# Group loads of the expert-value stage in four pieces, one behind each weight load

## The reference, cut to what matters

```python
act = jax.nn.gelu(jnp.einsum('cd,ced->ce', xc, expert_u[ic]), approximate=False)
return jnp.einsum('ce,ced->cd', (gc * act).astype(xc.dtype), expert_v[ic])
```

## Time and profile before

| | |
|---|---|
| time, median of 3 runs | 4268.71 us (4264.19 to 4283.66) |
| the profiled execution, span | 4269.1 us |
| TensorE matmul busy | 4033.2 us (94%) |
| VectorE busy | 2519.8 us (59%) |
| GpSimd busy | 2309.5 us (54%) |
| ScalarE busy | 1502.1 us (35%) |
| value stage, from its first matmul to its last | 3127 to 4244 us |
| DMAs from the stream, 1024 KB each | 396 |
| DMAs of gates, 704 KB each | 32 |
| DMAs of activations, 704 KB each | 32 |

### The profile page before, as it was taken

The page is one execution under the profiler, slowest core; times in us unless marked ns, Lnnn a source line. Parts: engine busy times, 40 slices in busy tenths (PEclk is TensorE's granted clock), DMA queues, the critical chain, the costliest instruction groups (busy, mean ns, idle before and its releaser), DMA issues.

```text
span 4269.1 us, 70172 instructions
## 1 busy us (share of the span) xinstructions
PE 4033.2 (94%) x27233; PEld 3579.2 (84%) x27233; DVE 2519.8 (59%) x3407; ACT 1502.1 (35%) x2053; POOL 2309.5 (54%) x930
## 2 busy tenths in 40 slices
PE   7999999999999999899998799999998999999997
PEld 5777777777788778699998799999988999999997
DVE  4344334444454552367773666667467788778775
ACT  4332323333322221233335766666322222222223
POOL 4332233333233443354555467667667888888774
PEclk9999999999999999999999999999999999999998
DMA  3222222222223343233334699999898999999893
GB/s 122 89 83 85 82 91 79 92 85 90 88 89 108 136 143 130 109 133 131 131 123 174 253 358 373 372 371 364 332 357 328 356 360 372 353 359 361 301 349 117
DMA packets 258397, 899.44 MB, mean 211 GB/s; under 512 B 107672, under 2 KB 140696, under 8 KB 162736
## 3 DMA queue, kind: packets, MB, share of 16 engines
q1 hardware_dynamic: 175984, 482.50, 32.0%
q0 software_dynamic: 46080, 335.56, 19.2%
q10 hardware_dynamic: 36160, 78.85, 4.8%
HBM read 828.10 MB, written 68.71 MB: 210 GB/s over the span
## 4 chain that ended last, share of the span: by engine, by line
PE 56%; issue 14%; POOL 9%; DMA 6%; ACT 5%; SPq 5%; DVE 3%; ACTq 1%; POOLq 0%; DVEq 0%
PE ps L389 14%; PE ps L391 13%; PE ps L390 13%; POOL wl L384 7%; DMA raw<-stream 5%; SPq L555 5%; PE ps L1985 2%; PE ps L1987 2%; PE ps L1986 2%; PE ps L1675 2%; ACT wh L380 2%; ACT stage L1038 1%; ACT oh L1033 1%; DVE stage L1470 1%; PE ps L1934 1%
## 5 line engine op out<-in xcount | busy, mean ns | idle before, releaser
L384 POOL TENSOR_TENSOR wl<-raw,wh 128x2048 fp32r<-128x2048 f32 x396 | 1834.6, 4633 | 1836.1 <-ACT wh L380 1835.7
L389 PE MATMUL ps<-xh,wh 128*128 128x352 f32 (+1 forms) x3904 | 1434.0, 367 | 37.6 <-DVE xl L1162 18.9
L391 PE MATMUL ps<-xh,wl 128*128 128x352 f32 (+1 forms) x3904 | 1400.8, 359 | 0.0
L390 PE MATMUL ps<-xl,wh 128*128 128x352 f32 (+1 forms) x3904 | 1399.3, 358 | 0.0
L380 ACT ACTIVATE wh<-raw 128x2048 fp32r<-128x2048 f32 x396 | 758.2, 1915 | 1595.1 <-PE ps L391 775.7
L389 PEld LDWEIGHTS ps<-xh,wh 128*128 128x128 f32 x3904 | 740.3, 190 | 133.6 <-issue 44.3
L391 PEld LDWEIGHTS ps<-xh,wl 128*128 128x128 f32 x3904 | 738.9, 189 | 83.4
L390 PEld LDWEIGHTS ps<-xl,wh 128*128 128x128 f32 x3904 | 740.4, 190 | 81.5 <-issue 7.7
L1985 PE MATMUL ps<-gah,wh 128*128 128x352 f32 x2048 | 682.7, 333 | 81.6 <-POOL wl L384 67.8
L1987 PE MATMUL ps<-gah,wl 128*128 128x352 f32 x2048 | 675.7, 330 | 0.0
L1986 PE MATMUL ps<-gal,wh 128*128 128x352 f32 x2048 | 674.0, 329 | 0.0
(11 more groups left out here) (333 smaller groups left out, 4020.1 us busy)
## 6 DMA issues: line engine op xcount, KB each, us to landing
raw<-stream SPq DMA_DIRECT2D x396, 1024.0 KB
gelu_scratch<-preb ACTq DMA_DIRECT2D x128, 176.0 KB
gates_scratch<-stage ACTq DMA_DIRECT2D x22, 1024.0 KB
gt<-gates_scratch SPq DMA_DIRECT2D x32, 704.0 KB
act<-gelu_scratch SPq DMA_DIRECT2D x32, 704.0 KB
mergegate_scratch<-sgb ACTq DMA_DIRECT2D x32, 256.0 KB, 2.1
sgm<-mergegate_scratch SPq DMA_DIRECT2D x32, 256.0 KB, 2.7
h_in<-x_t SPq DMA_DIRECT2D x4, 1024.0 KB, 9.0
```

Of the source, the lines that this page charges most:

```text
L384: pool.tensor_tensor(wl[s][:, :], raw[s][:, :], wh[s][:, :].bitcast(F32), ALU.subtract).then_inc(w_lo, 1)
L389: pe.matmul(dst, w_h, h[:, kx, lo:], start=start, stop=False)
L390: pe.matmul(dst, w_h, l[:, kx, lo:], start=False, stop=False)
L391: return pe.matmul(dst, w_l, h[:, kx, lo:], start=False, stop=stop)
```

## The change

`load_group` gets a part number. The gates are loaded in three pieces along their first axis (blocks 0 to 6, 7 to 13 and 14 to 21 of 22), the activations are the fourth piece. For a group g other than 0, the pieces of group g+2 are issued one behind each unit load of group g: gates behind c = 0, 1 and 2, activations behind c = 3. The waits that stood before the load (`gal_ready` of group g among them) now stand behind the unit load c = 0. For group 0 all four pieces stay together where the loads were, behind c = 2 (group 1) and c = 3 (group 2), and the load of group 0 itself is four pieces together. A group now raises `group_in` by 64, not 32. SP's loop over pairs of groups is written out (32 groups). The two raw buffers, and all that ACT, DVE, POOL and PE do, stay, but for the value that POOL waits for.

```diff
-            def load_group(g, s):
-
-                sp.dma_start(gt[s][:, :, :], gate_d[:, :, bass.ds(GE * g, GE), :].rearrange("b p e t -> p b (e t)")).then_inc(group_in[s], 16)
-                sp.dma_start(act_[s][:, :, :], act_d[bass.ds(GE * g, GE)].rearrange("e p t -> p e t")).then_inc(group_in[s], 16)
+            def load_group(g, s, part):
+                if part < 3:
+                    b = slice(GB * part // 3, GB * (part + 1) // 3)
+                    sp.dma_start(gt[s][:, b, :], gate_d[b, :, GE * g:GE * g + GE, :].rearrange("b p e t -> p b (e t)")).then_inc(group_in[s], 16)
+                else:
+                    sp.dma_start(act_[s][:, :, :], act_d[GE * g:GE * g + GE].rearrange("e p t -> p e t")).then_inc(group_in[s], 16)
...
-            load_group(0, 0)
+            for part in range(4):
+                load_group(0, 0, part)
...
                 for c in range(NC4):
                     load_unit(sp, U_PEER + NC4 * g + c, c % 2)
-                    if c == 3 and ahead:
+                    if c == 2 and first:
+                        sp.wait_ge(w_used, U_PEER)
+                        for part in range(4):
+                            load_group(1, 1, part)
+                    if c == (3 if first else 0) and ahead:
                         for r in range(2):
                             sp.wait_ge(pre_stored[r], 16 + 8 * NKEYS)
                         sp.wait_ge(gal_ready, GE * g + GE)
-                        load_group(g + 2, s)
-                    if c == 2 and first:
-                        sp.wait_ge(w_used, U_PEER)
-                        load_group(1, 1)
-
-            for s in range(2):
-                load_values(s, s, first=s == 0)
-            with sp.Fori(1, GROUPS // 2 - 1) as i:
-                for s in range(2):
-                    load_values(2 * i + s, s)
-            for s in range(2):
-                load_values(GROUPS - 2 + s, s, ahead=False)
+                    if ahead and (c == 3 or not first):
+                        for part in range(4) if first else (c,):
+                            load_group(g + 2, s, part)
+
+            for g in range(GROUPS):
+                load_values(g, g % 2, ahead=g < GROUPS - 2, first=g == 0)
...
             def gated(g, s, e):
-                pool.wait_ge(group_in[s], 16 * (g - s) + 32)
+                pool.wait_ge(group_in[s], 32 * (g - s) + 64)
```

## The result

The changed kernel takes 4256.2 us (median of 17), the kernel before, in the same rounds, 4274.0. The ratio is 0.9949, with a 95% interval of 0.9937 to 0.9961: 0.5% faster, where 1.1% was forecast. The time lies in the stated range; the gain is 18 us where 47 was forecast. Two of the 17 executions ran at a much lower granted clock (4932 and 5752 us at 0.75 and 0.63), and all ratios go by the others.

The account below looks back on a forecast made before the run. Late unit loads, queued behind the group load in one piece, were taken to bound the stage, not PE. 4269.1 - 50 (engines' share) + 3 (load of c = 1) = 4222 us; range for 8 in 10: 4190 to 4265.

Parts of the forecast that it names:

- What bounds the kernel: Value stage, groups 1 to 28: late unit loads set the pace, not PE; loss 115 us, DMA engines' work 897 us.
- The engines' term: Groups 1 to 28: smoothing raises the DMA share from 0.92 to 0.97, a gain of 50 us, bounds 21 to 78.
- (b): Load of c = 1, now behind the wait and first piece: 3 us added in all, bounds 0 to 53.
- (c): Groups before and after: group 0 keeps its loads and hold, groups 29 to 31 load nothing; cost 0.
- crowded case: Load of c = 1 beside gathers: packets take up to 7 us, landing at 11.0, PE loses 1.9 us a group.
- rival 3: At c = 0 the first piece holds SP as long as the whole did: 112 us slower, 4381; chance 0.07.
- (a): SP's queue: two more DMA issues a group, at most 1.3 us of SP's 34.8; cost nothing.
- (d): SP's loop written out: fewer register instructions, more instruction fetch; cost 0, bounds -1 to +2.
- (e): POOL's multiplications wait for four DMAs, not two; first use is some 20 us later, so no new wait.
- Rival 2: Engines already full: lateness spreads to all four units and the gathers, share stays 0.94; gain 19, 4250; chance 0.20.
- Rivals 1 and 4: First: engines can do more, only PE's pace is left, 4169, chance 0.08. Second: pieces bunch up as before, 4269, 0.03.
- The signs: Expected in the profile: L555 off the chain, ACT's 245 us of waits halved, clock 0.98, DMA share 0.96 to 0.98.

Follow-up runs that it names:

- one_later: Changed kernel with the wait and all pieces one unit load later (wait and first gates' piece behind c = 1); 4203.6 us, ratio to before 0.9824, repeat 0.9829.
- wait_alone: one_later with the wait behind c = 0 and the activations' piece issued before that wait; ratio to before 0.9874, repeat 0.9850.
- one_later_wait0: one_later with the wait behind c = 0 and the activations' piece after it, ahead of load c = 1; ratio to before 0.9976.
- two_at_0: Changed kernel with two gates' pieces behind c = 0, the third behind c = 1, activations behind c = 2; ratio to before 1.0032.
- group1_later: Changed kernel, but in group 1 alone the wait and first two gates' pieces stand behind c = 1; 4244.3 us, ratio to before 0.9928.
- split_only: Kernel before with the load cut in four pieces, all behind c = 3, and SP's loop written out; ratio to before 0.9980.
- act_first: Changed kernel with the activations' piece behind c = 0 and the gates' pieces behind c = 1, 2 and 3; ratio to before 0.9978.

## Why the prediction was wrong in size, point by point

**What bounds the kernel: right.** The stage was held by late units, not by PE, and the engines' work, 897 us, stayed (893). The chain and the DMA share gave it.

**The engines' term (-50): right in itself, but it is not this kernel's.** It says what well placed pieces bring. one_later has a share of 0.98 and gains 61.8 us in groups 1 to 28 (975.0 to 913.2), where I had put 50 and bounds of 21 to 78. The changed kernel reached 0.94 and 24.9 us; the 36.9 us between the two are the next terms, (b) and (c).

**The step that failed is (b), the load of c = 1, put at 3 us in all with bounds of 0 and 53. It measured 26.5 us over groups 2 to 28 (908.9 us against one_later's 882.4), and 36.9 us with group 1 (950.1 against 913.2).** What I wrote of its mechanism was there: the wait ends 0.4 us after the low half, the piece goes first. SP is not held for the 2.2 us that I had (a piece's issue takes 0.43 us in the median, as the row below shows), so the load is issued 0.9 us after its low half and not 3.2. But the piece's data goes ahead of the unit's, and the unit then takes 9.7 us to ACT, where I had 4.3 free and 7.8 crowded. Together that is 10.6 us in the median, near the 11.0 of my crowded case, not the 7.5 of the free one. The crowded case was the normal one, as the share of 0.92 said. I then took 3 us with the reason that the engines' shortage already counted it. That was upside down: the share comes out of the lateness. The 10.4 us of group 1 belong to (c) below. By the medians one_later is some 53 us faster; the profiled executions are 37 us apart, 4246.3 and 4209.4, since that of the changed kernel is the fastest of its 17 and that of one_later the slowest of its 5. That it was the piece behind the wait, and not the moving of all four, is shown by wait_alone against one_later_wait0 and by two_at_0. Two slips in the sum of (b) change nothing: 11.0 less 7.8 is 3.2, not 3.1, and the 2.5 us of slow clock in rival 3 stand in no row (rows 4 give 3.0).

The gates' pieces on SP's queue, all 96 (ns min/median/max; compare):

```profile
L555 SPq DMA_DIRECT2D gt<-gates_scratch x96: 367/434/14960, 3033.2 to 4116.3; - x96
```

**(c), no cost in the groups before and after: wrong in group 1.** I looked at where the pieces of group 0 stand and not at the wait of group 1, the first that stands at c = 0. There the last `gal` of group 1 comes late: POOL makes its last two products only at 3157.37 to 3159.23, and DVE takes a gathered row before the `gal` (SP's queue, DVE and PE, changed kernel):

```profile
3166.35 0.37 SPq L555 DMA_DIRECT2D gt<-gates_scratch  x1
3166.76 0.57 SPq L374 DMA_DIRECT2D raw<-stream  x1
...
3164.19 2.06 DVE L1487 TENSOR_TENSOR gal<-act,gah 128x352 fp32r<-128x352 f32 x2
...
3181.52 0.66 PE L1986 MATMUL ps<-gah,wh 128*128 128x352 f32 x1 [7.27 <-POOL wl L384]
```

The low half that releases the load of c = 1 ends at 3154.88, 11.9 us before the issue at 3166.76; PE stands 7.27 us and starts again at the lower clock (0.66 us a matmul). group1_later and the pairs of wait_alone and one_later put it at 8 to 9 us.

**(a), (d), (e) at nothing: right**, by split_only.

**The rivals.** Rival 2 (engines full, gain 19, 4250) is what the number looks like, but its reason falls: the engines were not full at 0.94, and PE's gaps stand mostly at c = 1, not at all four units. That it came within 6 us of the result is luck. The 358 GB/s of the Trainium skill's "DMA: Bandwidth & Descriptors" (section "Bandwidth"), which would have given 22 us of gain, is a like case: near the result by luck, and against the 379 GB/s that one_later moves over 710 us. I had left out that the same section gives this figure for two cores that stream from one memory; here one core runs. Rival 3 had the right place, the load c = 1, with the wrong mechanism, a hold of SP; two_at_0 shows that the same place can make the change slower than before. Rivals 1 and 4 did not come.

**The signs.** The hold at the activations' DMA left the chain, no piece in groups 2 to 23 held SP for more than 2.6 us, and the clock rose to 0.98, as written. The share stayed at 0.94, where 0.96 to 0.98 was written, and DVE's wait for gathers at 13.5 us (13.1 before). ACT's waits for units did not halve, they grew, and they are a poor sign: in one_later they are 282 us, at a gain three times as large.

**Open.** Group 29 takes 38.2 us in the profiled execution of the changed kernel and 37.2 in group1_later, which has the same order there; in before it takes 30.9, in one_later 33.8 and in act_first 32.4. In the changed kernel the loss is again at c = 1: the load is issued at 4109.40, 0.9 us after its low half, ACT starts on it 14.0 us later, and PE stands 5.90 us. Why it is so long just there is not shown. Nor is it settled by what measure (bytes, runs or DMAs) a piece costs, or why wait_alone, timed first, stood 0.5% above one_later, where the profiles differ by 7 us.

## What to carry to other kernels

When a load is cut up and spread over a queue, ask of each piece which due load it now stands in front of, and put the wait that frees its buffer behind the load that is due next, not ahead of it: moving the wait and the pieces by one place was worth 1.25%, more than twice the 0.5% of the change itself. With the shared engines above 0.9 of their time, take the crowded end of a landing time as the normal case, and don't let one term stand in for another because both have the same cause. Look at the first pass of a steady order by itself: a wait that cost nothing over 22 groups cost 8 to 9 us in group 1.

## What the runs showed of the hardware

Here the traffic of a second queue decided whether order within the first queue mattered. With gathers of full rows (share 0.91 to 0.99), 0, 224 and 448 KB of gates ahead of a due 1 MB load behind the same wait gave a loss of 0.6, 1.7 and 3.8 us a group at that unit, but 704 KB of activations only 2.4; with the gathers halved, the 224 KB cost next to nothing (0.4 us, against 0.3 with nothing ahead).

In one_later the DMA engines sustained 0.99 of their time and 379 GB/s over 710 us with unit loads, gathers, activations and gates in runs of 256 B.

Behind a gates' DMA of 22 x 128 runs of 256 B the issue of the activations' DMA took SP 9.3 us in the median. Cut in three and spaced by a unit load, the pieces were issued in 0.43 us each in the median, with one of 87 in groups 2 to 23 over 1 us (2.6). Cutting alone did not do it: the four pieces together behind c = 3 (split_only) took SP 10.5 us in the median of groups 2 to 23, the two DMAs of before 9.9, and where the changed kernel keeps the pieces together, in group 0, one took 15.0.

A VectorE instruction with two inputs in SBUF ended with the GpSimd instruction over it: of the 84 `gal` instructions of the changed kernel that overlap a low half, 83 end 0.4 us after it, after 0.6 to 6.6 us, where one without overlap takes 0.5 us in 42 of 44 cases. A wait for such a result was a wait for GpSimd.
